# A one-layer encoder in fp32 on one core: shift and scale weights in four quarters, x in two groups, and Fourier columns folded

## The reference, cut to what matters

```python
mod = silu(c) @ w_ada + b_ada             # six pieces: shift, scale, gate; twice
h = rms_norm(x, g_mix) * (1 + sc_m) + sh_m
z = h @ w_in                              # zb zc za (384 each), zf (256), zu zv (384 each)
ya = zb * conv3(zc * za)
yf = real(fft2(zf, over tokens and within 64 channels, ortho))
yc = gelu(zu) * (w_sp @ rms_norm(gelu(zv)) + b_sp)
x = x + gt_m * (concat(rms_norm of ya, yf, yc) @ w_out)
x = x + gt_f * expert_choice_moe(modulate(x), 16 experts)
out = rms_norm(x, g_final)
```

## Time and profile before

| | us |
|---|---|
| median of 3 runs (1514.19 to 1516.32) | 1515.03 |
| the profiled execution | 1515.15 |
| its span, first to last instruction | 1513.3 |
| PE busy / DVE busy / ACT busy | 1436.5 / 1032.3 / 775.0 |
| granted clock of PE, mean | 0.982 |

### The profile page before, as it was taken

The page is one execution under the profiler, slowest core; times in us unless marked ns, Lnnn a source line. Parts: engine busy times, 40 slices in busy tenths (PEclk is TensorE's granted clock), DMA queues, the critical chain, the costliest instruction groups (busy, mean ns, idle before and its releaser), DMA issues.

```text
span 1513.3 us, 22821 instructions
## 1 busy us (share of the span) xinstructions
PE 1436.5 (95%) x8639; PEld 1277.9 (84%) x8639; DVE 1032.3 (68%) x1449; ACT 775.0 (51%) x1020; POOL 158.1 (10%) x129
## 2 busy tenths in 40 slices
PE   2999999999999986999999999999999999999992
PEld 1787777887788866999999999999999999999992
DVE  3422533676769877777777777777777767777776
ACT  4422121523542324666656666666666666666564
POOL 2000000000000002021021021022022022022010
PEclk9999999999999997999999999999999999999996
DMA  9334344554242364687788788788778778778786
GB/s 331 107 113 126 115 150 150 188 180 181 90 120 57 133 240 156 219 275 245 244 265 244 257 257 249 256 260 251 254 245 266 254 243 267 253 241 263 250 280 241
DMA packets 217941, 322.20 MB, mean 213 GB/s; under 512 B 7452, under 2 KB 174440, under 8 KB 217896
## 3 DMA queue, kind: packets, MB, share of 16 engines
q1 hardware_dynamic: 208760, 294.70, 57.8%
q0 software_dynamic: 8064, 26.30, 7.4%
q10 hardware_dynamic: 1072, 0.59, 0.1%
HBM read 290.07 MB, written 31.49 MB: 212 GB/s over the span
## 4 chain that ended last, share of the span: by engine, by line
PE 83%; DVE 8%; ACT 3%; DMA 2%; SPq 1%; issue 1%; POOL 0%; POOLq 0%; DVEq 0%; ACTq 0%
PE ps L1589 25%; PE ps L1237 24%; PE ps L1587 10%; PE ps L1610 4%; PE ps L1602 4%; PE ps L1611 4%; PE ps L1603 4%; PE ps L1606 4%; PE ps L1592 1%; DVE wlo L2172 1%; PE ps L1578 1%; DVE idxu L2040 1%; SPq L631 1%; DVE vals L2038 1%; DVE aff L2041 1%
## 5 line engine op out<-in xcount | busy, mean ns | idle before, releaser
L1589 PE MATMUL ps<-xT,whi 128*128 128x384 f32 x2048 | 576.6, 356 | 1.6 <-DVE xT L2288 1.6
L2172 DVE TENSOR_TENSOR wlo<-raw,whi 128x2048 fp32r<-128x2048 f32 x191 | 435.3, 2292 | 193.1 <-ACT whi L1134 193.1
L1587 PE MATMUL ps<-xT,wlo 128*128 128x192 f32 x1792 | 455.3, 254 | 0.0
L1589 PEld LDWEIGHTS ps<-xT,whi 128*128 128x128 f32 x2048 | 367.9, 189 | 2.4 <-issue 1.9
L1134 ACT ACTIVATE whi<-raw 128x2048 fp32r<-128x2048 f32 x192 | 362.4, 1906 | 0.0
L1587 PEld LDWEIGHTS ps<-xT,wlo 128*128 128x128 f32 x1792 | 342.5, 191 | 0.0
L1237 PE MATMUL ps<-hT,wring 128*128 128x512 f32 x1224 | 289.7, 395 | 5.7 <-DVE hT L1720 5.7
L1237 PEld LDWEIGHTS ps<-hT,wring 128*128 128x128 f32 x1224 | 229.4, 190 | 58.8 <-DVE hT L1720 6.3
L1171 ACT ACTIVATE gu_l<-ps 128x384 f32<-128x384 f32 x128 | 62.9, 491 | 152.4 <-PE ps L1589 152.4
L1237 PE MATMUL ps<-wo,Yhl 128*128 128x512 f32 x576 | 135.5, 393 | 2.4 <-DVE Yhl L1862 1.0
L1237 PEld LDWEIGHTS ps<-wo,Yhl 128*128 128x128 f32 x576 | 106.9, 188 | 25.3 <-issue 2.1
(11 more groups left out here) (236 smaller groups left out, 1551.9 us busy)
## 6 DMA issues: line engine op xcount, KB each, us to landing
raw<-in_w_gate SPq DMA_DIRECT2D x64, 1024.0 KB, 4.8
raw<-in_w_up SPq DMA_DIRECT2D x64, 1024.0 KB, 5.6
raw<-in_w_down SPq DMA_DIRECT2D x64, 1024.0 KB, 5.5
wraw<-in_w_in SPq DMA_DIRECT2D x34, 512.0 KB, 6.0
wraw<-in_w_ada SPq DMA_DIRECT2D x32, 512.0 KB, 4.6
ada_w<-in_w_ada SPq DMA_DIRECT2D x16, 512.0 KB, 11.3
acc_d<-x SPq DMA_DIRECT2D x12, 512.0 KB, 2.7
h_d<-h SPq DMA_DIRECT2D x12, 512.0 KB, 3.9
```

The source lines that it names most:

```text
L1587: pe.matmul(out[:, 0:CAP], wlo[:, slot, w], xT[:, k, 0:CAP], start=False, stop=False, skip_group_check=True)
L1589: mm = pe.matmul(out[:, 0:2 * CAP], whi[:, slot, w], xT[:, k, :], start=k == 0, stop=k == KB - 1, skip_group_check=True)
L2172: dve.tensor_tensor(wlo[:, j % SPL, :], raw[:, j % RAW, :], whi[:, j % SPL, :].bitcast(F32), ALU.subtract).then_inc(w_split, 1)
```

## The change

- The shift and scale columns of w_ada come in four quarters of eight pieces of 256 KB, each for one pair of blocks of both groups; one semaphore counts four pieces. x's second group is loaded behind the first quarter. The small rows are issued by ACT, and w_spatial and the head constants at the end of ACT's start. `ada_mix`, `mod_columns` and `mod_drain` work by quarters, and PE, ACT and DVE each have a new order written out. ACT's root reads the sum of squares itself.
- In the first quarter 16 transposes of the identity stand between the products, 16 more before the first product of x.
- The Fourier input is folded on DVE (`fold`) to a quarter of the rows before the head transform: sums and differences of rows n, n + S/2 and their mirror rows, with the middle row apart in `middle`. The head transform has 18 matmuls of 128 columns for each sequence (with weights of 64 columns for the sample), the sequence transform half as many instructions as before. DVE's additions into AB are replaced by copies.
- ab0 comes behind zv1 and its ada products. wo 1 and wo 2 are split within the loop, behind za2 and zb2.

```diff
-WO_AHEAD = {("zb", 0): 5, ("zb", 1): 6, ("zc", 2): 7}
+AB_JOBS = (2, 1)
+WO_AHEAD = {("zb", 0): 5, ("zb", 1): 6, ("zc", 2): 7, ("za", 2): 1, ("zb", 2): 2}
 
 
 def z_steps(s):
 
 
-    order = ["zf0", "zf1", "zv0", "ab0", "zv1", "vt0", "zv2", "vt1", "zu0", "vt2", "zu1", "zu2", "zc0", "sv0", "za0", "zb0",
+    order = ["zf0", "zf1", "zv0", "zv1", "ab0", "vt0", "zv2", "vt1", "zu0", "vt2", "zu1", "zu2", "zc0", "sv0", "za0", "zb0",
 ...
-            out += [("dft", 0, 0), ("dft", 0, 1), ("dft", 0, 2), ("wo", 0), ("dft", 0, 3)]
-            out += [("wo", b) for b in (1, 2, 3, 4)]
+            out += [("dft", 0, 0), ("dft", 0, 1)] + [("wo", b) for b in (0, 3, 4)]
         else:
-            out += [("dft", 1, m) for m in range(TL[1] // 2)]
+            out.append(("dft", 1, 0))
 ...
-    AB = pair("AB", (168, 168), lambda w: [w // (2 * P), 2, 2, 2, P])
+    AB = [at("AB0", 168 * K, [2, 2, 2, 2, P]), at("AB1", 168 * K, [2, 2, 2, P])]
+    halves = pair("halves", (176, 172), lambda w: [2, 2, w // 2])
 ...
             load_x(0, 0)
-            load_x(0, 1)
             stream_until(stream[len(FIRST)])
-            for n in range(2 * KB):
-                half, k = n // KB, n % KB
-                if n == KB:
+            for q in range(KB // 2):
+                for k in range(KB):
+                    src = w_ada[P * k:P * (k + 1), 0:2 * D].rearrange("p (a q n) -> p a q n", a=2, n=AW)[:, :, q, :]
+                    sp.dma_start(ada_w[:, k // GT, q, k % GT, :].rearrange("p (a n) -> p a n", a=2), src
+                                 ).then_inc(ada_in[2 * q + k // GT], 16)
+                if q == 0:
+                    load_x(0, 1)
 ...
+                    if c[1] == 1:
+                        wait_filled(act, "zb", 0, 1, NG[0] - 1)
+                    if c[1] == 2:
+                        wait_filled(act, "zc", 0, 2, NG[0] - 1)
                     if c[1] == 5:
-                        wait_filled(act, "ab", 0, TL[0] // 2 - 1, 1)
+                        wait_filled(act, "ab", 0, 1, 1)
 ...
-                act.wait_ge(var_x, tt // GT + 1)
-                act.activation(rsx[:, tt:tt + GT], rsx[:, tt:tt + GT], ACT.Sqrt).then_inc(std_x, 1)
+                act.wait_ge(ones_set, 2)
+                act.wait_ge(ssx_ready, tt + GT)
+                act.activation(rsx[:, tt:tt + GT], ssx[:, tt:tt + GT], ACT.Sqrt, bias=eps[:, :], scale=1.0 / D
+                               ).then_inc(std_x, 1)
 
             def hT_drains(s, g, pairs):
 
-                act.wait_ge(gsm_ready, 2 if pairs.stop <= 2 else 4)
+                act.wait_ge(gsm_ready, 2 * pairs.stop)
 ...
-                w_out_hi(3)
+                w_out_hi(1)
 ...
-            for g in range(NG[0]):
-                x_stats(0, g)
+            x_stats(0, 0)
             split_next(len(FIRST))
-            for half in range(2):
-                for g in range(NG[0]):
-                    hT_drains(0, g, range(2 * half, 2 * half + 2))
-                if not half:
-                    split_next()
+            hT_drains(0, 0, range(0, 1))
+            x_stats(0, 1)
+            hT_drains(0, 0, range(1, 2))
+            hT_drains(0, 1, range(0, 2))
+            hT_drains(0, 0, range(2, 3))
+            split_next()
+            hT_drains(0, 1, range(2, 3))
+            hT_drains(0, 0, range(3, 4))
+            hT_drains(0, 1, range(3, 4))
+            act.dma_start(wsp6[:, :, :], a["w_spatial"][0].rearrange("h p q -> p h q")).then_inc(wsp_in, 16)
+            act.dma_start(chs[:, :, :], a["dft_head"]).then_inc(small_in, 16)
 ...
+            def keep_clock(name, n):
+
+                for _ in range(n):
+                    pe.transpose(bank(name)[:, 0:P], ident[:, :], ident[:, :])
+
+            def ada_mix(q):
+
+                open_bank("adam", q)
                 for k in range(KB):
-                    pe.wait_ge(ada_in[KB * half + k], 16)
+                    if q == 0:
+                        keep_clock("warm0", 2)
+                    pe.wait_ge(ada_in[2 * q + k // GT], 16 * GT)
                     for j in range(4):
-                        ins = mm(ada_bank("adam", half)[32 * j:32 * (j + 1), :], silw[:, k, :],
-                                 ada_w[:, k // GT, half, k % GT, AW * j:AW * (j + 1)], k == 0, k == KB - 1)
-                fill(ins, "adam", half)
-
-            def mod_columns(half):
-
-                open_bank("mod", half)
-                wait_drained(pe, "adam", half)
-                for m in range(2):
-                    tr = pe.transpose(ada_bank("mod", half)[:, P * m:P * (m + 1)], stage_m[:, half, P * m:P * (m + 1)],
-                                      ident[:, :])
-                fill(tr, "mod", half)
+                        ins = mm(ada_bank("adam", q)[32 * j:32 * (j + 1), 0:P], silw[:, k, :],
+                                 ada_w[:, k // GT, q, k % GT, P * j:P * (j + 1)], k == 0, k == KB - 1)
+                fill(ins, "adam", q)
+
+            def mod_columns(q):
+
+                open_bank("mod", q)
+                wait_drained(pe, "adam", q)
+                fill(pe.transpose(ada_bank("mod", q)[:, 0:P], stage_m[:, q, :], ident[:, :]), "mod", q)
 ...
+            def head_dft(s):
+
+                quarter, rows = W[s] // 4, W[s] // 8
+                pe.wait_ge(small_in, 16 * 2)
+                pe.wait_ge(folded, 8 * (s + 1))
+                for par in range(2):
+                    for n in range(AB_JOBS[s]):
+                        out = open_bank("ab", s, par, n)
+                        for q in range(2) if s else (n,):
+                            for ab in range(2):
+                                for fb in range(2):
+                                    first = quarter * (2 * q + ab) + par
+                                    if s:
+                                        cols = slice(P * (2 * q + fb), P * (2 * q + fb + 1))
+                                        at_row = rows * (1 - ab)
+                                    else:
+                                        cols = slice(P * (2 * ab + fb), P * (2 * ab + fb + 1))
+                                        at_row = 0
+                                    more = par == q == 0 and ab == 1
+                                    ins = mm(out[at_row:at_row + rows, cols],
+                                             zfT[s][:, fb, first:first + 2 * rows - 1:2], chs[:, ab, :], True, not more)
+                                    if more:
+                                        ins = mm(out[0:32, cols], middle[:, fb, :], chs[:, 0, :], False, True)
+                        fill(ins, "ab", s, par, n)
 ...
+                quarter = W[s] // 4
                 for par, name in enumerate(("even", "odd")):
                     out = [open_bank(name, s, fb) for fb in range(2)]
-                    for c in range(chunks * par, chunks * (par + 1)):
-                        n = raw_n["dft", s, c]
-                        wait_drained(pe, "ab", s, c, 1)
-                        pe.wait_ge(ws_in[n % RS], 16 * (n // RS + 1))
-                        first, last = c == chunks * par, c == chunks * (par + 1) - 1
-                        for fb in range(2):
-                            for q in range(2):
+                    n = raw_n["dft", s, 0 if s else par]
+                    for q in range(AB_JOBS[s]):
+                        wait_drained(pe, "ab", s, par, q)
+                    pe.wait_ge(ws_in[n % RS], 16 * (n // RS + 1))
+                    for fb in range(2):
+                        for q in range(2):
+                            if s:
+                                at_col = quarter * (2 * par + q)
+                                ins = mm(out[fb][:, quarter * q:quarter * (q + 1)], AB[1][:, par, q, fb, :],
+                                         wraw[:, n % RS, at_col:at_col + quarter], q == 0, True)
+                            else:
                                 for ab in range(2):
-                                    at_col = half * q + quarter * ab
-                                    ins = mm(out[fb][:, quarter * q:quarter * (q + 1)], AB[s][:, c, q, fb, ab, :],
-                                             wraw[:, n % RS, at_col:at_col + quarter], first and q == ab == 0, last and ab == 1)
-                            if last:
-                                fill(ins, name, s, fb)
-                        if not last:
-                            ins.then_inc(dft_used, 1)
+                                    at_col = quarter * (2 * q + ab)
+                                    ins = mm(out[fb][:, quarter * q:quarter * (q + 1)], AB[0][:, par, q, ab, fb, :],
+                                             wraw[:, n % RS, at_col:at_col + quarter], q == ab == 0, ab == 1)
+                        fill(ins, name, s, fb)
 ...
+            x_blocks(0, 0, 0, 2)
+            pe.wait_ge(silw_ready, 1)
+            open_bank("warm0")
+            ada_mix(0)
+            mod_columns(0)
+            x_blocks(0, 0, 2, 4)
+            keep_clock("warm0", 16)
```

(76 more changed lines are left out.)

226 lines of the change are left out of this document (97 added, 129 removed).

## The result

| | before | after |
|---|---|---|
| median (lowest to highest), us | 1516.34 (1514.19 to 1517.13) | 1520.70 (1519.97 to 1523.51) |
| profiled execution: time, span | 1515.15, 1513.3 | 1523.51, 1521.7 |

The ratio is 1.0032, 95% interval 1.002 to 1.0044. By the medians that is 4.4 us slower, where I had forecast 1.65 us faster and a range that ended at 1519.5. The profiled execution of after is the longest of its six; a second one, taken later (after_again), took 1519.54 with a span of 1517.7, and both are used.

A forecast was written before the change was run, and what follows sets the result against it. PE was taken to bound the kernel, only the first 560 us counting. Start 4.8 + 1.55, Fourier -2.9 - 6.7, swap wait 2.0, sample -0.2, x_norm -0.2 gave -1.65 us: 1513.5, range 1507.5 to 1519.5.

The forecast's parts named there:

- The size of the start: Prompt's start: z's loop at 76.95 us instead of 72.12, +4.8, plus 1.55 for one fall of the clock.
- First quarter full at 26.5: First quarter's ada products: two visits at half clock (1.0 us each), six at 0.56, filled at 26.5 us.
- Second product: Second product of x with w_in, behind the second group's squares: at 41.85 us, taking 4.3 at half clock.
- The two waits for hT: Start, hT pairs standing on DVE behind a quarter's columns: 2 x 2.08 us, one clock fall of 1.55.
- Head transform: Prompt's head transform on PE: 36 instructions in 3.9 us instead of 6.83, so -2.9 us.
- The new wait behind the swap: Prompt, PE at vt0: waits for one gelu, then one gelu and one copy, +2.0 us (bounds 0 and 3).
- The fold: DVE, prompt: 5.9 us, starting 12 us into the stage, ending at 18, needed at 25; hidden at twice the price.
- the rival of an uncovered fold: Sample: backward reads at three times the price delay the router product by 3.3 us, 1516.8 in all; chance 0.05.
- The splits of wo 1 and wo 2: Prompt, queues of SP, ACT and DVE at za2 and zb2: nothing; at most a load, 4 us, without cover.
- The sample's half: Sample's ab -1.3 us, less router wait and swap: net -0.2, bounds -1.5 and +1.7; shorter sequence transform 0.
- the slower one: Start: weight pieces take time by packet, second product 4.45 us later, clock falling at both stalls: 1519.5 us; chance 0.12.
- What would show it: Start: first product near 31, second near 42, two hT waits of 2 us, z's loop from 77 us.

The follow-up runs named there:

- no_filler: After without the 16 filler transposes between the first quarter's eight visits (the 16 behind them stay): 1517.32 us, ratio to before 0.9999.
- order_hT: After with VectorE's start reordered, second group's hT pairs 1 and 2 ahead of the third and fourth quarters' shift and scale: 1512.54 us, ratio to before 0.9968.
- no_middle: Before with the Fourier part, sample's sequence transform computed twice, middle products left out: prompt's head transform 3.88 us for 32 products.
- swap_back: fold_only with ab0 ahead of zv1 again in the prompt, the sample keeping the changed order: 1513.29 us, ratio to before 0.9975.
- best_halves: fold_only with the sample's sequence transform computed twice, ab0 ahead of zv1 in the prompt, fold ahead of zv0's weight split: 1507.55 us, ratio to before 0.9943.
- fold_only: Before with the Fourier part of the change alone, the start keeping its halves: 1511.54 us, ratio to before 0.9963.
- tuned: After without fillers between the first quarter's visits, with VectorE's order as in order_hT and the sample's sequence transform computed twice: 1509.68 us, ratio to before 0.9948.

## Why the prediction was wrong, step by step

**What bounds it** held: TensorE carries the chain from the first product to the experts, and what was lost in the start is found again at w_out, less what the Fourier part gave back. A small slip of reading: of the 40 slices only 15 and 16 are under nine tenths inside the first 560 us, slice 14 is full.

**The size of the start** is the step that failed. I had seen its waits but summed it to +6.35 with the one fall of the clock; measured were +11.3 in after_again. With it every gain of the Fourier part was outweighed. The terms, forecast and after_again:

- First quarter full at 26.5, measured 28.3 (30.2 in the other run). I let two of eight visits pass at half pace, and priced entering and leaving the 32-column form at 0.13 us. At full pace a visit took 0.73 us, of which the two transposes are 0.22 and the eight products 0.22: 0.29 for the change of form. A visit at half pace took 1.2 us; three were in after_again, seven in the other run. +1.8. The Trainium skill, "TensorEngine Tiling (Array Packing)", Key Properties, says that a change of the tiling mode drains the engine. The trace agrees in so far as the change costs time, 0.29 us there and back or 2.3 us over eight visits, where I had 1.0. By no_filler nothing was gained for it.
- Second product: the wait for the second group's squares, which begin when ScalarE has done the first hT pair, was as I had it, carried along 1.8 late (43.69 for 41.85); the product itself took 5.0 us instead of 4.3. +0.7.
- The two waits for hT: seen, and sized well (1.96 each). I let the clock fall behind one of them; it fell behind both, in each of the six profiles that have them. +1.6. order_hT shows the cause and that nothing else stands behind it.
- The rest, +0.8: 0.5 of it are the other six products, which at the full clock took 2.81 to 2.94 us where I had read 2.77 off one row. The waits for stage_m (0.57 twice) were in my sum.

Together 4.9 us. **Head transform:** -1.9 for -2.9; the middle products are the difference, by no_middle. **Sequence transform:** 6.83 us for 6.9, right. **The new wait behind the swap:** 0.84 + 1.28 = 2.12 for 2.0, at the engines I had named, right. What I missed is its price beyond itself: in three of ten profiles the clock fell behind it, 1.6 us. **The fold** took 5.0 us for 5.9 and was hidden where I put it, but as swap_back and best_halves show only because the swap hid it; it could have started 9 us earlier (73.68 in best_halves, 83.02 in fold_only). Its instructions that read backwards took 0.68 us, no more than I had priced, so that the rival of an uncovered fold falls. **The splits of wo 1 and wo 2** I had put at nothing, because the same pattern at wo 5, 6 and 7 cost nothing. It is a wait after all, in nine of the thirteen profiles with these splits, 0.15 to 2.00 us (none in after, 0.86 in after_again, 2.00 in tuned), and by the path that I had named, the load of zb2 behind wo 1:

```profile
264.48 1.23 DVE L1724 TENSOR_TENSOR wo<-wraw,wo 128x1024 fp32r<-128x1024 f32 x1 [5.33 <-ACT wo L874]
265.73 0.38 SPq L650 DMA_DIRECT2D wraw<-in_w_in  x1
269.88 1.06 ACT L874 ACTIVATE wring<-wraw 128x1024 fp32r<-128x1024 f32 x1 [5.51 <-DMA wraw<-in_w_in]
270.98 1.23 DVE L1724 TENSOR_TENSOR wring<-wraw,wring 128x1024 fp32r<-128x1024 f32 x1 [5.28 <-ACT wring L874]
272.35 11.14 PE L1277 MATMUL ps<-hT,wring 128*128 128x512 f32 x48 [0.86 <-DVE wring L1724]
```

SyncE issues the load of zb2's weights only when the split of wo 1 has freed its slot, at 265.7 us, and they are split at 272.2; TensorE, done with its ada products at 271.5, begins 0.86 us late.

**The sample's half:** the head transform took 3.14 for 3.56, -0.4 (its four middle products again); no router wait came. My "0, DVE ends it" for the sequence transform was right for the idle time (2.79 for 0.99, with a transform 1.8 shorter) and wrong in what the idle time does: behind 1.0 us the clock held, behind 2.8 it fell in some runs, up to 2.9 us. The warning was in my own rows, which showed 1.0 us harmless and 2.2 us not; I used them for the start and not here.

The rest closes it: -1.65 + 4.9 + 1.0 + 0.9 (split) - 0.3 (transform and swap) - 0.8 (the experts' stretch, 921.3 us for 922.2, which is inside its spread and so chance) = +4.05, measured +4.4. That the sum closes is partly luck, since it holds for this pair of profiles: after and before differ by 8.4 us in the spans of their first profiles and by 2.5 in those of their second. Of the rivals, the slower one (1519.5) came nearest for the wrong reason: the pieces of 256 KB took no time by the packet (the transposes began at 19.5, forecast 19.3, and no_filler's 64 products ran without a wait). "What would show it" named the loop from 77; it came at 83 to 85, and the second product at 44 to 46, not 42.

## What to carry to other kernels

Removing TensorE work just ahead of a wait can cost time: count not only the wait that stays but whether its new length is one behind which the clock can fall, and if so, keep the engine at work or bring the late engine forward. When a stage is cut finer, write each in-order engine's list down beside the new list of TensorE: here VectorE idled 8 us while the block wanted next stood behind the one it waited for, and two moved lines were worth 7.0 us, more than the whole change had promised. Fillers between products of another form cost the change of form each time, and here hid nothing. Before blaming a part for 3 us, profile the same program twice: here the two profiles of after differ by 4.0 us.

## What the runs showed of the hardware

- **The clock behind a wait is partly chance.** Over sixteen profiled runs: behind 0.97 to 1.35 us for Yhl it never fell (nine of nine); behind 2.74 to 3.15 us at the same place it fell in four of seven (18 products in 5.7 to 7.2 us instead of 4.35); behind 2.2 us ahead of the sample's first z product in twelve of sixteen (4.5 us for 12 products instead of 3.0); behind 0.84 and 1.28 us with four transposes between, in three of ten; behind the hT waits of 1.96 us in twelve of twelve. Ahead of the first z product it was low behind 3.5 us in seven of seven. But the length of the wait alone does not decide: behind 2.04 us ahead of the head transform in swap_back and behind 2.00 us for a weight split in tuned it held (48 products in 11.2 us). What decides a single case stays open.
- **At the beginning of its work TensorE ran at about half pace with a granted clock recorded as 1.00**, for 3 to 6 us and once for 10: in after, pairs of transposes took 0.69 instead of 0.44 us up to 29 us, and the window shows

```profile
21.30:29.00 7.70, 7.70 (x63) 3.18 (x62) 0.44 (x1) 0.00 (x0) 0.00 (x0) 1.00 1.06 375
```

  In this stretch only the durations tell. The pace rose between 22.5 and 24.6 us in four runs of an identical start and at 29 us in the fifth.
- **A change between instructions with weights of 128 and of 32 columns cost 0.3 us there and back**, by the visits (0.29) and by no_middle (1.05 us for two visits of two products of 0.11: 0.30 each). Between weights of 64 and of 32 columns, in the sample, it is 0.37 (1.18 us for two visits, less the same 0.44).
